# Spatial gating bias: a DVE addition from a copy on every partition in place of one-row TensorE products

## The chip, the cores and the metric

The kernel runs on one core of a Trainium2 chip. The metric is the device time in microseconds. Engines are called PE (TensorE), DVE (VectorE), ACT (ScalarE), POOL (GpSimd) and SP (SyncE). PE writes its products to PSUM, eight banks of 512 fp32 values on each of 128 partitions; the other engines read them from there.

## What is computed

One block of a first network (S5 branch, spatial gating branch, memory attention, feed-forward part) is followed by two layers of a second one (two attentions, a dense feed-forward part, eight experts), for 256 positions of width 1024. The change touches the spatial gating branch only:

```
def sgu_branch(zu, zv, ln_g, ln_b, w_s, bias):
    zu = jax.nn.gelu(zu)
    zv = layer_norm(jax.nn.gelu(zv), ln_g, ln_b)
    zv = zv.reshape(bsz, seq // CHUNK, CHUNK, SGU_HEADS, SGU_HEAD_DIM)
    sv = jnp.einsum('hts,bnshd->bnthd', w_s, zv) + bias.T[None, None, :, :, None]
    return zu * sv.reshape(bsz, seq, SGU_WIDTH)
```

There are 8 heads of 128 columns and 2 chunks of 128 positions. The bias has one number for each head and position, the same for all 128 columns of a head.

## The kernel before

Each engine has one instruction list, written in the order of the computation. The weights come as a stream of 1 MB chunks that SP loads into `ring`, seven slots; PE's first product with a chunk releases a slot, and SP loads the next chunk into it. The results of PE are numbered as units, and unit n lies in PSUM bank n mod 8. `open_unit` waits until the bank's previous unit is free, `close_unit` marks the unit full, `take_unit` waits for that on the engine that reads it, and `free_unit` and `evacuated` signal and wait for the end of the reading. `link` on DVE marks an instruction's end on a semaphore and has DVE wait for it.

Around the change PE runs these stages in order: the transposes and small products of the S5 branch, the projections zu, ga, gb and k (`form_a`, line 657), the projection v (`form_b`, line 683), the spatial gating products (units `sgu` 0 to 3), the projection pb (`form_a`, line 657, with the gated `zuT` as its moving operand), and the y products of the S5 branch (lines 972 to 989). Each projection is four chunks.

The gating works transposed: partitions are the columns of a head, the free axis is the position. A unit `sgu` u holds two heads with two chunks each, four blocks of 128x128. For each block PE makes the product of `zv` with the mixing matrix in `sguT` (L955) and adds to the same bank a product that is one row deep, ones times the bias row `sbias` (L956). `sbias` is one partition of `yaT`, a region that the memory's transpose (`memT`) uses until the projection v has read it, so ACT issues its load (L1466) behind v's last evacuation (L1293). DVE multiplies each unit with `zuT` in place (L2008). Before that, DVE runs the S5 scan (L1984 to L1990, in a loop) up to a small memset (L2001); the scan's data lie in `big`. PE waits for the fourth gated unit before pb.

Of the kernel before, what the change touches and what calls it, by code (L numbers as in the profile page):

```python
# [31 lines left out]
P = 128  # L32
TOK = 256
TB = TOK // P
D = 1024
# [6 lines left out]
ALU = mybir.AluOpType  # L42
# [203 lines left out]
def build(nc, a, out):  # L246
    with ExitStack() as ctx:
# [31 lines left out]
        ones = sb("ones", [P, P])  # L279
# [7 lines left out]
        with ExitStack() as early:  # L287
# [3 lines left out]
            sguT = region("sguT", [P, 8, P])  # L291
            big = region("big", [P, 16384])
# [44 lines left out]
        def view(region, lo, size, pat, **kw):  # L337
# [21 lines left out]
        zv = view(r_zv, 0, 2048, "p (b d) -> p b d", b=TB)  # L359
# [3 lines left out]
        v_t = view(r_v, 0, 2048, "p (b d) -> p b d", b=TB)  # L363
        ygT = memT[:, 0:4, :]
        yaT = memT[:, 4:8, :]
        sbias = yaT.rearrange("p a t -> p (a t)")

        prob = view(r_zv, 0, 1024, "p (n b m) -> p n b m", n=2, b=TB)
        probT = view(r_zv, 1024, 1024, "p (n b l) -> p n b l", n=2, b=TB)
# [31 lines left out]
        loads = {n: sem("ld_" + n) for n in (  # L401
            "x", "mem", "ident", "gains", "prm", "b", "lnv", "sgu", "sbias", "s5d", "cw", "bgate", "sink",
            "nab", "bc0", "ln1", "ln2", "consts")}
# [62 lines left out]
        def bank(u):  # L466
            return psum[:, UNIT_AT[u] % BANKS, :]
# [9 lines left out]
        def take_unit(eng, u):  # L477
            n = UNIT_AT[u]
            eng.wait_ge(bank_full[n % BANKS], n // BANKS + 1)

        def free_unit(last, u):
            last.then_inc(bank_free[UNIT_AT[u] % BANKS], 1)

        def evacuated(eng, u):

            n = UNIT_AT[u]
            eng.wait_ge(bank_free[n % BANKS], n // BANKS + 1)
# [40 lines left out]
        n = 0  # L528
# [89 lines left out]
        def _(pe):  # L618
# [272 lines left out]
            for u in range(8):  # L891
                open_unit(pe, ("t_b", u))
                for j in range(4):
                    n = 4 * (u % 4) + j
                    last = nc.tensor.transpose(bank(("t_b", u))[:, j * P:(j + 1) * P],
                                               b_wide_f[u // 4][:, n * P:(n + 1) * P], ident[:, :])
# [5 lines left out]
            for u0 in range(0, BLK // 2, 4):  # L902
# [3 lines left out]
                for j in range(2):  # L906
                    for r in range(2):
                        for n in (1, 0):

                            for u in group:  # L910
# [6 lines left out]
                                last = nc.tensor.matmul(bank(("bu", u))[:, (2 * j + r) * SCAN:(2 * j + r + 1) * SCAN],  # L917
                                                        bT[n][r0:r0 + 32, r * 8 + blk // 4, :],
                                                        earlier if n else later, start=(n == 1), stop=(n == 0))
# [5 lines left out]
            for d in range(2):  # L925
                for pair in range(PAIRS):
                    i, q = pair % 4, pair // 4
                    for r in range(2):
                        last = nc.tensor.matmul(bank(("kmat", 0))[32 * i:32 * i + 32, (4 * d + q) * 32:(4 * d + q + 1) * 32],
                                                b_wide[0][:, r, d * PAIRS + pair, :, :].rearrange("p g c -> p (g c)"),  # L930
                                                cw[:, r, d * PAIRS + pair, :], start=(r == 0), stop=(r == 1))
# [12 lines left out]

            pe.wait_ge(zvn_ready, 1)
            pe.wait_ge(loads["sgu"], 16)
            pe.wait_ge(loads["sbias"], 16)
            pe.wait_ge(ones_ready, 1)
            for u in range(4):
                open_unit(pe, ("sgu", u))  # L950
                for j in range(2):
                    hd = 2 * u + j
                    for b in range(TB):
                        o = bank(("sgu", u))[:, j * TOK + b * P:j * TOK + (b + 1) * P]
                        nc.tensor.matmul(o, zv[:, b, hd * P:(hd + 1) * P], sguT[:, hd, :], start=True, stop=False)  # L955
                        last = nc.tensor.matmul(o, ones[0:1, :], sbias[0:1, hd * P:(hd + 1) * P],  # L956
                                                start=False, stop=True)
                close_unit(last, ("sgu", u))
            evacuated(pe, ("sgu", 3))
            for i in range(4):  # L960
# [4 lines left out]
            for q in range(4):  # L965
# [3 lines left out]
                for odd in range(2):  # L969
                    for i in range(4):  # L970
                        rows = slice(32 * i, 32 * i + 32)
                        nc.tensor.matmul(out[i][odd], kmat[rows, odd, q, :], uT[rows, q, odd::2],
                                         start=(odd == 0), stop=False, skip_group_check=True)
                for odd in range(2):
                    for r in range(2):
# [5 lines left out]
                        for i in range(4):  # L981

                            fwd, bwd = 4 * q + i, PAIRS + 4 * q + i
                            if odd:
                                last = nc.tensor.matmul(out[i][1][:, 0:SCAN - 1], cw_lam[:, r, bwd, :],
                                                        states[:, SCAN - 2::-1, r, bwd], start=False,
                                                        stop=(r == 1), skip_group_check=True)
                            else:
                                last = nc.tensor.matmul(out[i][0][:, 1:SCAN], cw_lam[:, r, fwd, :],
                                                        states[:, 0:SCAN - 1, r, fwd], start=False,  # L990
                                                        stop=(r == 1), skip_group_check=True)
# [27 lines left out]
            for m in range(2):  # L1019

                for b in range(TB):
# [4 lines left out]
                    for i in range(2):  # L1026
                        if b == 0:
                            open_unit(pe, (f"projb{m}", i))
                        last = split_b_block((f"projb{m}", i), ("k8", f"w_in_{m}", i), b, b)
# [10 lines left out]
                for u in range(3):  # L1040
                    open_unit(pe, (f"t_sw{m}", u))
                    for j in range(2 if u < 2 else 1):
                        for b in range(TB):
                            last = nc.tensor.transpose(
                                bank((f"t_sw{m}", u))[:, (2 * j + b) * P:(2 * j + b + 1) * P],
                                qk_t[:, b, (2 * u + j) * P:(2 * u + j + 1) * P], ident[:, :])
# [39 lines left out]
            for b in range(TB):  # L1086
# [3 lines left out]
                for k in range(KD):  # L1090
                    last = nc.tensor.matmul(bank(("router", 0))[:, b * 8:(b + 1) * 8], xT[:, k, b * P:(b + 1) * P],
                                            wr[:, k, :], start=(k == 0), stop=(k == KD - 1))
# [147 lines left out]
        def _(act):  # L1240
# [198 lines left out]
            for u in range(8):  # L1439
                take_unit(act, ("t_b", u))  # L1440
                n = 4 * (u % 4)
                last = nc.scalar.activation(bT[u // 4][:, n:n + 4, :],
                                            bank(("t_b", u)).rearrange("p (n m) -> p n m", m=P), ACT.Copy)
                free_unit(last, ("t_b", u))
            for u in range(0, BLK // 2, 2):
                take_unit(act, ("bu", u))
                last = nc.scalar.activation(states[:, :, :, bu_block(u):bu_block(u) + 5:4].rearrange("p t r k -> p k r t"),
                                            bank(("bu", u)).rearrange("p (k r t) -> p k r t", k=2, r=2), ACT.Copy)
                free_unit(last, ("bu", u))
            take_unit(act, ("kmat", 0))  # L1450
            last = nc.scalar.activation(kmat[:, :, :, :].rearrange("p d q m -> p (d q m)"),
                                        bank(("kmat", 0))[:, 0:256], ACT.Copy)
            free_unit(last, ("kmat", 0))
            for i in range(4):
                out_of(("zu", i), zuT[:, 2 * i:2 * i + 2, :], ACT.Gelu_apprx_tanh)
            for i in range(4):
# [6 lines left out]
            for i in range(4):  # L1463
                out_of(("v", i), v_t[:, :, i * 256:(i + 1) * 256], ACT.Copy)

            act.dma_start(sbias[0:1, :], a["sgu_bias"]).then_inc(loads["sbias"], 16)  # L1466
            for q in range(4):
                evacuated(act, ("y", q))
                nc.scalar.activation(ygT[:, q, :], ygT[:, q, :], ACT.Gelu_apprx_tanh).then_inc(yg_ready, 1)
            for i in range(2):  # L1470
                take_unit(act, ("glu", i))
                last = nc.scalar.activation(yaT[:, 2 * i:2 * i + 2, :], halves(bank(("glu", i))), ACT.Sigmoid)
# [24 lines left out]
            for m in range(2):  # L1497
# [15 lines left out]
                u = (f"projb{m}", 4)  # L1513
# [3 lines left out]
                last = nc.scalar.activation(v_sw, halves(bank(u))[:, :, 128:256], ACT.Copy)  # L1517
# [19 lines left out]
                for u in range(3):  # L1537
# [3 lines left out]
                    else:  # L1541
                        last = nc.scalar.activation(ksT, bank((f"t_sw{m}", u))[:, 0:TOK], ACT.Copy)
# [94 lines left out]
        def _(dve):  # L1637
# [3 lines left out]
            def link(ins):  # L1641

                steps[0] += 1
                ins.then_inc(dve_step, 1)
                dve.wait_ge(dve_step, steps[0])
# [356 lines left out]


            evacuated(dve, ("zu", 3))
            for u in range(4):
                take_unit(dve, ("sgu", u))
                zs = zuT[:, 2 * u:2 * u + 2, :]
                last = V.tensor_tensor(zs, zs, halves(bank(("sgu", u))), ALU.mult)  # L2008
                free_unit(last, ("sgu", u))
# [429 lines left out]
```

## Time and profile before

| | |
|---|---|
| three runs | 2306.70, 2312.81, 2315.01 us; median 2312.81 |
| profiled execution | 2305.68 us, span 2303.90 us |
| PE busy | 2160.8 us, 94% of the span |
| DVE busy | 1559.0 us, 68% |
| ACT busy | 1193.2 us, 52% |
| granted PE clock, mean | 0.968 of full speed |

PE's lines count two records for each fp32 product. An engine's busy share is a mean over stages with different limits, so the stage around the change is read by itself.

### The profile page before, as it was taken

The page shows a single profiled execution, that of the slowest core. Times are in us where ns is not written, and L with a number is a line of the kernel's source. Part 1 is how long each engine was busy: PE and PEld are TensorE (multiplying, and loading weights), DVE is VectorE, ACT ScalarE, POOL GpSimd, SP SyncE. Part 2 cuts the span into 40 slices and gives each one's busy share as a digit, 9 for nine tenths or more (in the row PEclk, how much of TensorE's full clock was granted, in tenths as well). Part 3 has the DMA queues.
Part 4 walks back from the last instruction along what each step waited for, and adds up shares of the span by engine and source line. Part 5 has one row for each costly group of instructions (what it writes and reads, how often), then busy time and mean ns, then how long its engine had stood idle before and what let it go on. Part 6 is the DMA issues. An engine that isn't in the chain of part 4 may idle for free.

```text
span 2303.9 us, 33192 instructions
## 1 busy us (share of the span) xinstructions
PE 2160.8 (94%) x12622; PEld 1886.0 (82%) x12622; DVE 1559.0 (68%) x1741; ACT 1193.2 (52%) x1203; POOL 9.8 (0%) x22
## 2 busy tenths in 40 slices
PE   6999998799989889998989899999999999999997
PEld 6888778699979688998968788888888888888885
DVE  6775125444554744445474788989898989989897
ACT  2311033344434824343481577777777777777775
POOL 0000000000000000000000000000000000000000
PEclk9999899899999999999999799999999999999998
DMA  7243233245554244555424498989898989989894
GB/s 294 93 149 143 73 121 116 73 166 187 192 205 165 76 145 175 190 184 201 165 74 147 194 372 347 364 343 366 344 366 352 363 344 363 365 345 364 352 358 165
DMA packets 76288, 541.50 MB, mean 235 GB/s; under 512 B 9121, under 2 KB 9265, under 8 KB 11810
## 3 DMA queue, kind: packets, MB, share of 16 engines
q1 hardware_dynamic: 72128, 524.32, 59.2%
q0 software_dynamic: 2080, 10.40, 1.3%
q10 hardware_dynamic: 1986, 5.41, 0.6%
q8 instruction: 73, 1.20, 0.2%
q14 instruction: 21, 0.17, 0.0%
HBM read 539.05 MB, written 1.05 MB: 234 GB/s over the span
## 4 chain that ended last, share of the span: by engine, by line
PE 88%; DVE 6%; ACT 4%; issue 2%; DMA 0%; DVEq 0%; ACTq 0%
PE psum L1173 13%; PE psum L817 11%; PE psum L1150 9%; PE psum L1154 9%; PE psum L1153 9%; PE psum L657 7%; PE psum L716 6%; PE psum L704 6%; PE psum L830 4%; PE psum L670 3%; PE psum L683 2%; PE psum L1116 2%; PE psum L1162 1%; ACT wp_h L1374 1%; PE psum L979 1%
## 5 line engine op out<-in xcount | busy, mean ns | idle before, releaser
L2169 DVE TENSOR_TENSOR w_l<-ring,w_h 128x2048 fp32r<-128x2048 f32 x338 | 773.4, 2290 | 115.9 <-ACT w_h L1360 109.2
L1360 ACT ACTIVATE w_h<-ring 128x2048 fp32r<-128x2048 f32 x338 | 647.6, 1916 | 139.5 <-PE psum L1150 96.1
L1150 PE MATMUL psum<-w_h,xe_h 128*128 128x512 f32 x896 | 360.1, 402 | 2.4 <-DVE xe_l L2253 2.4
L1154 PE MATMUL psum<-w_h,xe_l 128*128 128x512 f32 x896 | 350.8, 391 | 0.0
L1153 PE MATMUL psum<-w_l,xe_h 128*128 128x512 f32 x896 | 350.3, 391 | 0.0
L1820 DVE TENSOR_TENSOR wf_l<-ring,wf_h 128x2048 fp32r<-128x2048 f32 x66 | 151.2, 2291 | 156.9 <-ACT wf_h L1351 156.9
L1794 DVE TENSOR_TENSOR wp_l<-ring,wp_h 128x2048 fp32r<-128x2048 f32 x52 | 119.1, 2292 | 162.3 <-ACT wp_h L1374 162.3
L817 PE MATMUL psum<-xf_h,wf_h 128*128 128x256 f32 x704 | 201.2, 286 | 4.5 <-DVE xf_l L1812 2.5
L817 PE MATMUL psum<-xf_l,wf_h 128*128 128x256 f32 x704 | 200.9, 285 | 0.0
L817 PE MATMUL psum<-xf_h,wf_l 128*128 128x256 f32 x704 | 200.8, 285 | 0.0
L1150 PEld LDWEIGHTS psum<-w_h,xe_h 128*128 128x128 f32 x896 | 168.8, 188 | 38.3 <-DVE w_l L2169 4.0
L1154 PEld LDWEIGHTS psum<-w_h,xe_l 128*128 128x128 f32 x896 | 168.7, 188 | 36.2
L1153 PEld LDWEIGHTS psum<-w_l,xe_h 128*128 128x128 f32 x896 | 169.2, 189 | 32.3
L1351 ACT ACTIVATE wf_h<-ring 128x2048 fp32r<-128x2048 f32 x66 | 125.9, 1910 | 113.7 <-PE psum L830 58.5
L1374 ACT ACTIVATE wp_h<-ring 128x2048 fp32r<-128x2048 f32 x52 | 99.4, 1914 | 145.5 <-PE psum L716 75.2
L817 PEld LDWEIGHTS psum<-xf_h,wf_h 128*128 128x128 f32 x704 | 136.9, 194 | 5.9 <-DVE xf_l L1812 2.8
L1173 PE MATMUL psum<-w_h,eT_h 128*128 128x512 f32 x448 | 140.0, 394 | 0.0
L1173 PE MATMUL psum<-w_h,eT_l 128*128 128x512 f32 x448 | 138.4, 390 | 0.0
L1173 PE MATMUL psum<-w_l,eT_h 128*128 128x512 f32 x448 | 138.2, 390 | 0.0
L817 PEld LDWEIGHTS psum<-xf_l,wf_h 128*128 128x128 f32 x704 | 136.9, 194 | 0.7
L716 PE MATMUL psum<-wp_h,xf_h 128*128 128x256 f32 x384 | 113.1, 295 | 25.7 <-DVE xf_l L1828 12.8
L817 PEld LDWEIGHTS psum<-xf_h,wf_l 128*128 128x128 f32 x704 | 136.8, 194 | 0.0
(366 smaller groups left out, 3721.6 us busy)
## 6 DMA issues: line engine op xcount, KB each, us to landing
ring<-in_stream SPq DMA_DIRECT2D x499, 1024.0 KB, 5.3
big<-in_bc POOLq DMA_DIRECT2D x11, 512.0 KB, 7.0
big<-in_na_bias POOLq DMA_DIRECT2D x2, 2048.0 KB, 9.4
h<-in_x SPq DMA_DIRECT2D x1, 1024.0 KB, 7.2
big<-in_mem ACTq DMA_DIRECT2D x1, 1024.0 KB, 8.6
r_k<-in_sgu_ln ACTq DMA_DIRECT2D x1, 1024.0 KB, 22.5
big<-in_s_c ACTq DMA_DIRECT2D x1, 1024.0 KB, 29.7
out_dram<-ysum ACTq DMA_DIRECT2D x1, 1024.0 KB, 4.1
```

What stands on the lines that cost most here:

```text
L657: last = nc.tensor.matmul(bank(unit)[:, j * TOK:(j + 1) * TOK], w[:, k, j * P:(j + 1) * P], act_T[:, k, :], start=(k == 0), stop=(k == KD ...
L704: last = nc.tensor.matmul(bank(unit)[:, j * TOK:(j + 1) * TOK], w[:, k, j * P:(j + 1) * P], x[:, k, :], start=(k == i == 0), stop=(k == KD ...
L716: last = nc.tensor.matmul(bank(unit)[:, at * 256:(at + 1) * 256], x[:, k, b * P:(b + 1) * P], w[:, k, :], start=(k == i == 0), stop=(k == ...
L817: last = nc.tensor.matmul(psum[:, ff_bank(name, b), j * TOK:(j + 1) * TOK], w[:, k, j * P:(j + 1) * P], x[:, k, :], start=(k == i == 0), s ...
L1150: first = nc.tensor.matmul(out, xe_h[:, k, :], wh[:, i, :], start=(k == 0), stop=False)
L1153: nc.tensor.matmul(out, xe_h[:, k, :], wl[:, i, :], start=False, stop=False)
L1154: last = nc.tensor.matmul(out, xe_l[:, k, :], wh[:, i, :], start=False, stop=(k == KD - 1))
L1173: last = nc.tensor.matmul(psum[:, 4 + c, :], x[:, s % 2, k, :], w[:, k, c * 512:(c + 1) * 512], start=(s == 0 and k == n == 0), stop=(s == ...
L1351: nc.scalar.activation(wf_h[:, n % SPLITS, :], ring[:, at % SLOTS, :], ACT.Copy).then_inc(wf_high, 1)
L1360: nc.scalar.activation(high, src, ACT.Copy).then_inc(w_high, 1)
L1820: V.tensor_tensor(wf_l[:, n % SPLITS, :], ring[:, at % SLOTS, :], wf_h[:, n % SPLITS, :].bitcast(F32), ALU.subtract).then_inc(wf_split, 1)
L2169: V.tensor_tensor(low, src, high.bitcast(F32), ALU.subtract).then_inc(w_split, 1)
```

## The change

The bias is loaded to all 128 partitions, into 1024 columns of `big` that the small S5 products have no more use for, and by ACT ahead of the zu evacuations. PE makes only the sixteen mixing products. DVE adds the bias to each unit in PSUM and then multiplies. PE no longer waits for the bias, DVE does.

```
-        sbias = yaT.rearrange("p a t -> p (a t)")
+        sbias = big[:, 8192:9216].rearrange("p (n m) -> p n m", m=P)
...
             pe.wait_ge(zvn_ready, 1)
             pe.wait_ge(loads["sgu"], 16)
-            pe.wait_ge(loads["sbias"], 16)
             pe.wait_ge(ones_ready, 1)
             for u in range(4):
                 open_unit(pe, ("sgu", u))
                 for j in range(2):
                     hd = 2 * u + j
                     for b in range(TB):
-                        o = bank(("sgu", u))[:, j * TOK + b * P:j * TOK + (b + 1) * P]
-                        nc.tensor.matmul(o, zv[:, b, hd * P:(hd + 1) * P], sguT[:, hd, :], start=True, stop=False)
-                        last = nc.tensor.matmul(o, ones[0:1, :], sbias[0:1, hd * P:(hd + 1) * P],
-                                                start=False, stop=True)
+                        last = nc.tensor.matmul(bank(("sgu", u))[:, j * TOK + b * P:j * TOK + (b + 1) * P],
+                                                zv[:, b, hd * P:(hd + 1) * P], sguT[:, hd, :], start=True, stop=True)
                 close_unit(last, ("sgu", u))
...
             free_unit(last, ("kmat", 0))
+
+            act.dma_start(big[:, 8192:9216], a["sgu_bias"].to_broadcast([P, D])).then_inc(loads["sbias"], 16)
             for i in range(4):
                 out_of(("zu", i), zuT[:, 2 * i:2 * i + 2, :], ACT.Gelu_apprx_tanh)
...
-            act.dma_start(sbias[0:1, :], a["sgu_bias"]).then_inc(loads["sbias"], 16)
             for q in range(4):
                 evacuated(act, ("y", q))
...
             evacuated(dve, ("zu", 3))
+            dve.wait_ge(loads["sbias"], 16)
             for u in range(4):
                 take_unit(dve, ("sgu", u))
+                gate = bank(("sgu", u)).rearrange("p (j b m) -> p j b m", j=2, b=TB)
+                link(V.tensor_tensor(gate, gate, sbias[:, 2 * u:2 * u + 2, :].unsqueeze(2).to_broadcast([P, 2, TB, P]),
+                                     op=ALU.add))
                 zs = zuT[:, 2 * u:2 * u + 2, :]
                 last = V.tensor_tensor(zs, zs, halves(bank(("sgu", u))), ALU.mult)
                 free_unit(last, ("sgu", u))
```

PE, from the end of the projections k and v to the start of pb (`r_zv` holds `zv`, `memT` in L956 is `sbias`, `r_zu` holds `zuT`):

```order
 L657 MATMUL psum<-memT,ring 128x256 x64
 L683 MATMUL psum<-ring,memT 128x256 x64
-L955 MATMUL psum<-sguT,r_zv 128x128
-L956 MATMUL psum<-memT,ones 128x128
...
+L953 MATMUL psum<-sguT,r_zv 128x128 x16
 L657 MATMUL psum<-r_zu,ring 128x256 x64
```

The pair L955, L956 stood sixteen times; sixteen products follow each other now, under the line number 953. Nothing else on PE moves.

DVE, from the end of the scan to the product with pb, before (`r_gb` holds `gbT`):

```order
L1987 TENSOR_TENSOR scan_t<-scan_t 128x64
L1990 TENSOR_TENSOR big<-scan_t,big 128x64
L2001 MEMSET msq 128x2
L2008 TENSOR_TENSOR r_zu<-r_zu,psum 128x512 x4
L2014 TENSOR_TENSOR r_gb<-r_gb,psum 128x512 x4
```

and in the changed kernel:

```order
L1985 TENSOR_TENSOR scan_t<-scan_t 128x64
L1988 TENSOR_TENSOR big<-scan_t,big 128x64
L1999 MEMSET msq 128x2
L2007 TENSOR_TENSOR psum<-psum,big 128x512
L2010 TENSOR_TENSOR r_zu<-r_zu,psum 128x512
...
L2016 TENSOR_TENSOR r_gb<-r_gb,psum 128x512 x4
```

The addition L2007 stands ahead of each of the four products L2010, which were L2008.

ACT, from the last copy of the S5 set-up on, in the changed kernel:

```order
L1444 ACTIVATE big<-psum 128x2x2x128 x8
L1448 ACTIVATE kmat<-psum 128x256
L1452 DMA big<-in_sgu_bias 128x1024
L1290 ACT_TABLE_LOAD
L1290 ACTIVATE r_zu<-psum 128x512 x4
```

The load of the bias stood behind the evacuations of v before, as `memT<-in_sgu_bias` of one row, and now stands ahead of those of zu.

## Rows read from the trace of the kernel before

**Rows 1.** The page: busy time by engine, and the chain by engine.

```profile
PE 2160.8 (94%) x12622; PEld 1886.0 (82%) x12622; DVE 1559.0 (68%) x1741; ACT 1193.2 (52%) x1203; POOL 9.8 (0%) x22
...
PE 88%; DVE 6%; ACT 4%; issue 2%; DMA 0%; DVEq 0%; ACTq 0%
```

**Rows 2.** The chain in order of time: start us, us, what.

```profile
197.82 27.63 PE psum L683 x128
225.44 1.63 issue
...
228.78 0.42 PE psum L955 x2
229.20 0.72 PE psum L956 x2
...
248.76 0.70 DVE r_zu L2008
249.50 29.61 PE psum L657 x128
```

**Rows 3.** The timeline: start us, us, engine, line, what, [idle before it].

```profile
72.11 2.48 DVE L1713 SCALAR_TENSOR_TENSOR r_zv<-r_zv,rstd,r_k 128x1024 f32<-128x1024 f32 x2
...
87.70 1.28 ACT L1293 ACT_TABLE_LOAD   x1
94.25 0.60 ACT L1293 ACTIVATE r_zu<-psum 128x512 f32<-128x512 f32 x1 [5.27 <-PE psum L657]
...
215.78 0.23 DVE L1990 TENSOR_TENSOR big<-scan_t,big 128x64 f32 x1 [0.15 <-DVE scan_t L1987]
...
218.05 0.06 DVE L2001 MEMSET msq<- 128x2 f32 x1
...
225.49 0.49 ACTq L1466 DMA_DIRECT2D memT<-in_sgu_bias  x1
```

**Rows 4.** Groups of instructions, 225.4 to 249.6 us, busy us, mean ns, idle.

```profile
L956 PE MATMUL psum<-memT,ones 1*128 1x128 f32 x32 | 12.1, 475 | 0.0
L955 PE MATMUL psum<-sguT,r_zv 128*128 128x128 f32 x32 | 11.8, 468 | 1.6 <-issue 1.6
...
L2008 DVE TENSOR_TENSOR r_zu<-r_zu,psum 128x512 f32<-128x512 f32 x4 | 2.8, 688 | 28.6 <-PE psum L956 28.6
```

**Rows 5.** Windows: length, PE, PEld, DVE, ACT, POOL busy, clock, DMA share, GB/s.

```profile
227.07:229.12 2.05, 2.05 (x10) 1.45 (x10) 0.00 (x0) 0.31 (x1) 0.00 (x0) 1.00 0.00 0
229.12:248.73 19.61, 19.61 (x55) 13.47 (x54) 2.06 (x3) 0.00 (x0) 0.00 (x0) 0.50 0.00 0
...
249.50:253.00 3.50, 3.50 (x8) 2.86 (x9) 0.00 (x0) 0.00 (x0) 0.00 (x0) 0.50 0.27 61
253.00:279.05 26.05, 26.05 (x122) 22.61 (x120) 2.06 (x3) 0.00 (x0) 0.00 (x0) 1.00 0.42 154
```

**Rows 6.** DMA issues: out<-in, queue, count, KB each, us to landing.

```profile
ring<-in_stream SPq DMA_DIRECT2D x499, 1024.0 KB, 5.3
big<-in_bc POOLq DMA_DIRECT2D x11, 512.0 KB, 7.0
...
r_k<-in_sgu_ln ACTq DMA_DIRECT2D x1, 1024.0 KB, 22.5
```

**Rows 7.** Windows around two later gaps of PE, columns as in rows 5.

```profile
316.00:317.00 1.00, 0.09 (x1) 0.00 (x0) 0.24 (x1) 0.87 (x2) 0.00 (x0) 1.00 0.99 414
317.00:318.00 1.00, 0.49 (x2) 0.47 (x3) 0.45 (x1) 1.00 (x1) 0.00 (x0) 1.00 0.96 386
...
333.00:334.00 1.00, 0.00 (x0) 0.00 (x0) 0.91 (x3) 0.63 (x1) 0.00 (x0) 1.00 0.00 0
...
335.00:336.00 1.00, 1.00 (x7) 1.00 (x7) 0.00 (x0) 0.00 (x0) 0.00 (x0) 0.50 0.00 0
```

**Rows 8.** Groups of instructions, whole span: two of DVE with 128x512 elements.

```profile
L1974 DVE COPY big<-psum 128x512 f32<-128x512 f32 x8 | 9.6, 1310 | 3.3 <-PE psum L917 3.1
...
L1940 DVE TENSOR_TENSOR r_v<-r_zu 128x512 f32<-128x512 f32 x4 | 2.8, 692 | 0.1
```

More of the change, by code:

```diff
@@ L365, in build @@
         yaT = memT[:, 4:8, :]
-        sbias = yaT.rearrange("p a t -> p (a t)")
+        sbias = big[:, 8192:9216].rearrange("p (n m) -> p n m", m=P)
         prob = view(r_zv, 0, 1024, "p (n b m) -> p n b m", n=2, b=TB)
@@ L946, in _ @@
             pe.wait_ge(loads["sgu"], 16)
-            pe.wait_ge(loads["sbias"], 16)
             pe.wait_ge(ones_ready, 1)
@@ L953, in _ @@
                     for b in range(TB):
[L954 to L957, printed above, removed]
+                        last = nc.tensor.matmul(bank(("sgu", u))[:, j * TOK + b * P:j * TOK + (b + 1) * P],
+                                                zv[:, b, hd * P:(hd + 1) * P], sguT[:, hd, :], start=True, stop=True)
                 close_unit(last, ("sgu", u))
@@ L1453, in _ @@
             free_unit(last, ("kmat", 0))
+            act.dma_start(big[:, 8192:9216], a["sgu_bias"].to_broadcast([P, D])).then_inc(loads["sbias"], 16)
             for i in range(4):
@@ L1464, in _ @@
                 out_of(("v", i), v_t[:, :, i * 256:(i + 1) * 256], ACT.Copy)
-            act.dma_start(sbias[0:1, :], a["sgu_bias"]).then_inc(loads["sbias"], 16)
             for q in range(4):
@@ L2004, in _ @@
             evacuated(dve, ("zu", 3))
+            dve.wait_ge(loads["sbias"], 16)
             for u in range(4):
                 take_unit(dve, ("sgu", u))
+                gate = bank(("sgu", u)).rearrange("p (j b m) -> p j b m", j=2, b=TB)
+                link(V.tensor_tensor(gate, gate, sbias[:, 2 * u:2 * u + 2, :].unsqueeze(2).to_broadcast([P, 2, TB, P]),
+                                     op=ALU.add))
                 zs = zuT[:, 2 * u:2 * u + 2, :]
```

## The prediction

> **What bounds the kernel now.** I began with the page's busy table and its chain. TensorE (PE) is busy 94% of the span and carries 88% of the chain, DVE 6% of it [rows 1]. So an instruction taken off PE pays only where PE itself is the chain, and one put on DVE costs only where PE waits for DVE. Next I read the chain around the spatial gating [rows 2]. It runs from the end of the projection of v (L683) at 225.44 us to the first product of the next projection (L657) at 249.50 us, 24.06 us in three pieces:
> - 1.63 us in which PE issues nothing, 225.44 to 227.07. In the timeline [rows 3] the ACT queue issues the one-row load of sgu_bias (L1466) at 225.49, right after PE ended. Of PE's four waits there, the one for `loads["sbias"]` alone has a producer that isn't long done: the layer norm behind `zvn_ready` ended at 74.6 us, and `sguT` and the ones come from the first instructions. The profile doesn't name the releaser ("issue"), so that it is this load is my reading.
> - 21.66 us of 32 products, each of which shows as two PE records. 16 are L955 (the 128x128 mixing matrices), 16 are L956 (the bias, one row deep). The groups show that the two cost the same, 468 and 475 ns a record [rows 4]: the one-row product isn't cheaper for having one row. In the chain a product takes 0.42 us up to 229.20 us, and behind it 27 of them take 229.20 to 248.76, 0.72 us each [rows 2].
> - 0.77 us for the last DVE product of the stage (L2008, 0.69 us) and its two handovers.
>
> The step from 0.42 to 0.72 us is the clock. The granted clock is 1.00 up to 229.12, then 0.50, PE's lower level (1.2 of 2.4 GHz), until 253.00 [rows 5]. Ahead of the fall stood the 1.63 us gap and five products. It rose again 3.5 us into the 256-column products of L657. PE has work without a pause from 229.12 to 248.73, and still the clock stays low.
>
> **The change, part by part.**
>
> *The load moves.* It is issued by ACT behind the kmat copy at about 87.7 us, and PE no longer waits for it. It grows from 4 KB to 512 KB (128 partitions by 4 KB). Loads of that kind and size take 7.0 us to land, and the slowest broadcast of the trace 22.5 us, in the crowd of the first microseconds [rows 6]. DVE wants it after its scan, at 218.05 at the earliest [rows 3]: over 100 us of cover. On ACT the issue lies ahead of a table load at 87.70, and ACT's next evacuation starts at 94.25 [rows 3], so some 5 us of idle time hide it. On the rings it is half of one 1 MB weight chunk; PE eats one chunk per 6.9 us in such a projection (27.63 us for the four of L683) [rows 2] and seven slots stand ahead of it. Cost nothing; if all cover failed, a chunk would be late by about half its 5.3 us [rows 6], 2.7 us. Gain: the 1.63 us.
>
> *Sixteen products leave.* What is left is 16 products of L953. At the upper clock: 16 x 0.42 = 6.7 us. At the lower one throughout: 16 x 0.724 = 11.6 us. Which of them holds is the largest unknown. Before the change PE had the 1.63 us gap and then 2.05 us of this work when the clock fell, 3.68 us after 225.44. Now the work follows the projection without a gap. If the clock fell at the same 229.12 all the same, 8.8 products would be done, and the other 7.2 take 5.2 us: 8.9 us for the sixteen. I take 7.8 us, the middle between never falling (6.7) and falling at the old moment (8.9). For staying up speaks that a later gap of about that length, between 316 and 318 us, didn't bring it down between dense products, while one of nearly 3 us ahead of 334.5 did [rows 7]; for falling speaks that this sparse work never raised it in 19.6 us.
>
> A rule that would shrink this: the Trainium skill gives 134 cycles at the upper clock for 128 columns, 56 ns ("TensorE: Matmul & The Clock Gate", section Back-to-back issue gap), and four passes for true FP32 ("FP8 and Floating Point Precision", section TensorE Precision Notes). That is an estimate of 0.22 us a product; this trace doesn't agree, with 0.42 us. By the Trainium skill's pages the sixteen would be worth 3.6 us.
>
> *Four DVE additions come in.* Each is a 128x512 fp32 tensor_tensor that reads PSUM and the copy (a stride-0 repeat over the two blocks) and writes back to PSUM. Reading PSUM costs nothing extra in the rows (L2008 688 ns), nor does a repeated operand (L1940, 692 ns) [rows 4, 8]. No row of the trace has DVE write PSUM. Below, I bound it by 0.69 us, or 0.60 if it were like ACT's 128x512 evacuations [rows 3]; above, by the slowest group of 128x512 on DVE, the permuting copy L1974 at 1.31 us [rows 8]. I take 0.69, the nearest in shape and operation. The `link` between addition and product costs 0.15 us, the idle ahead of L1990 in the scan, which has the same wait on DVE's own semaphore [rows 3]. A unit thus takes DVE 0.69 + 0.15 + 0.69 = 1.53 us, while PE makes its four products in 1.68 us or more: three of the four pairs lie under PE's work. DVE stands idle for over 28 us of this stage now [rows 4]. Only the last pair is exposed: 0.03 + 1.53 + 0.05 = 1.6 us instead of 0.77. Behind it queue the four products of L2014, which wait for PE anyway. At 1.31 us an addition, DVE would be the pace: first unit ready at 1.68, then 4 x 2.15 us, 10.3 us in all.
>
> *Sum.* Now 24.06 us; after 0 + 7.8 + 1.6 = 9.4 us. Gain 14.7 us, between 15.8 (clock up) and 13.6 (clock falls at the old moment). The projection behind it has about 3.5 us at the lower clock before [rows 5]; with the longer pause of 1.6 us ahead of it I expect about the same. Nothing later reclaims the time: the weight stream is moved by PE's own releases, and its DMA share is 0.42 even behind this stage, at the upper clock [rows 5]. The profiled execution took 2305.68 us (span 2303.90, 1.8 us around it), so 2291.0 us by its own measure. It is at the low end of the runs shown (2306.70 to 2315.01), so against the median of 2312.81 the same gain gives **2298 us**.
>
> **The rivals.**
> - *The clock is low from the first product.* 11.6 + 1.6 = 13.2 us, gain 10.9, 2302 us. For it: in 19.6 us this kind of work never raised the clock. Against it: PE comes out of dense work at 1.00 with no gap. Chance 0.10.
> - *DVE sets the pace,* as PSUM writes are slow. 10.3 us at the upper bound with the clock up, and 8.9 + 2.2 = 11.1 with its fall at the old moment: gain 13.8 or 13.0, about 2299.5 us. For it: the kernel has never had DVE write PSUM. Against it: L2008 and L1940, of the same shape and kind, take 0.69 us whether they read PSUM or SBUF [rows 4, 8]. Chance 0.10.
> - *The products were cheap.* If only the streaming time of a removed product comes back, half of a 256-column product of L683 (27.63 us / 64 = 0.432), that is 16 x 0.216 = 3.5 us, and the gain is 1.63 + 3.5 - 0.83 = 4.3 us: 2308.5 us. Speaks against it that L955 and L956 alternate at equal spacing. The Trainium skill's price of a product gives much the same sum. Chance 0.03.
> - *PE still waits,* since the 1.63 us gap has another cause, such as the switch from one bank to the next. Gain 14.7 - 1.6 = 13.1 us, 2299.7 us. Against it: the chain shows no such gap where one projection follows another. Chance 0.05.
> - *Slower: the clock stays down.* With 6.7 us of sparse work and a longer pause, PE could be at the lower level through the next projection too. At 1.00 that takes about 27.7 us (64 products at 0.432), so at 0.50 it costs 27.7 us more, less the 1.75 us it loses now: 26 us, net 11.3 us slower, 2324 us. It decides from 14.7 us on, that is, from 29 us at the lower clock. Against it: the clock rose 3.5 us into the same products, from the same low level. Chance 0.02.
> - *The gain is there but the whole shows less.* Everything behind moves forward by 15 us and meets the clock's falls at other moments; three runs of the same kernel differ by 8.3 us. Net gain under 11.6 us. Chance 0.12.
>
> My forecast has the rest, 0.58.
>
> **How the numbers follow.** From no change a measurement can tell about 0.5%, 11.6 us. The forecast (0.58) lies above it; so do, with the scatter, 0.08 of the DVE pace, 0.04 of the waiting PE and 0.02 of the low clock: faster 0.72. Same: the rest of those, the cheap products, and the whole that shows less: 0.26. Slower: 0.02. For the range: the gain is 10.9 to 15.8, and up to 17.5 if the next projection loses nothing to the clock; the median of a few runs moves by some 4 us around that. 2312.8 - 17.5 - 4 = 2291 and 2312.8 - 10.9 + 4 = 2306. The forecast's own range is 2293 to 2303.
>
> **What the profile after would show.** No idle time between L683 and L953, and no DMA issue there. 32 records of L953, spaced 0.21 us while the clock reads 1.00 and 0.36 at 0.50; the fall, if there is one, in the middle of them or behind them. L2007 four times at about 0.69 us; each pair but the last inside PE's products. From the end of L683 to the first L657 behind it 8.3 to 10.5 us. The scan and the zu, ga, gb stages unchanged. The prediction is wrong if PE still waits at the start, if L953 runs at 0.36 us from its first record, or if L2007 takes over 1 us.

## The result and the profile after

| | before | after |
|---|---|---|
| six runs each, median | 2310.56 us | 2287.35 us |
| lowest to highest | 2306.47 to 2315.01 | 2285.48 to 2296.66 |
| ratio of the times | | 0.9904 [0.9888, 0.9919] |
| profiled execution | 2305.68 us, span 2303.90 | 2285.48 us, span 2283.7 |
| granted PE clock, mean | 0.968 | 0.974 |
| end of L683 to first L657 of pb | 24.06 us | 6.49 us |

The changed kernel is 0.96% faster by the ratio, 22 us; the two medians are 23.2 us apart. Both are more than the forecast of 14.7 us, and the median lies 3.7 us below the low end of the range of 2291 to 2306 us. The page after, where [rows 1] stood before:

```profile
PE 2140.5 (94%) x12590; PEld 1873.3 (82%) x12590; DVE 1560.0 (68%) x1745; ACT 1193.1 (52%) x1203; POOL 9.8 (0%) x22
```

The chain after, over the stretch of [rows 2] (start us, us, what):

```profile
197.86 27.63 PE psum L683 x128
225.49 0.91 PE psum L953 x8
226.39 0.03 issue
226.42 0.05 DVEq L479
226.47 0.04 issue
226.52 0.71 DVE psum L2007
227.23 0.02 issue
227.25 0.69 DVE r_zu L2010
227.94 0.62 DVE psum L2007
...
231.24 0.70 DVE r_zu L2010
231.94 0.04 issue
231.98 29.58 PE psum L657 x128
```

The pause ahead of the products is gone. Only the first unit of PE is in the chain, and it is there for 0.91 us with four products (eight records). From 226.52 us on the chain is DVE's, four pairs of addition and product at 1.33 us each. The groups between 225.4 and 232.1 us (busy us, mean ns of a record, idle before), where [rows 4] stood:

```profile
L953 PE MATMUL psum<-sguT,r_zv 128*128 128x128 f32 x32 | 3.7, 275 | 0.0
...
L2007 DVE TENSOR_TENSOR psum<-psum,big 128x512 f32<-128x512 f32 x4 | 2.8, 694 | 8.4 <-PE psum L953 8.4
L2010 DVE TENSOR_TENSOR r_zu<-r_zu,psum 128x512 f32<-128x512 f32 x4 | 2.7, 687 | 0.1
```

Sixteen products take 3.7 us by busy time and 3.57 us by the window below, that is 0.22 to 0.23 us each and not 0.42. The mean of a record, 275 ns, is longer than its spacing, since records overlap: a price is read from busy time or from the chain. The windows, to be set beside [rows 5]:

```profile
225.49:229.06 3.57, 3.57 (x32) 3.38 (x31) 2.48 (x4) 1.88 (x2) 0.00 (x0) 1.00 0.00 0
229.06:231.98 2.92, 0.00 (x0) 0.00 (x0) 2.80 (x5) 0.00 (x0) 0.00 (x0) 1.00 0.00 0
231.98:232.86 0.88, 0.88 (x4) 0.80 (x5) 0.00 (x0) 0.00 (x0) 0.00 (x0) 1.00 0.00 0
232.86:236.28 3.42, 3.42 (x10) 2.71 (x9) 0.00 (x0) 0.00 (x0) 0.00 (x0) 0.50 0.64 220
236.28:261.56 25.28, 25.28 (x121) 21.98 (x124) 2.06 (x3) 0.00 (x0) 0.00 (x0) 1.00 0.38 137
```

The granted clock is 1.00 during all sixteen products and during the 2.92 us in which PE waits for DVE. It falls 0.9 us into pb and is up again 3.42 us later. The load of the bias, in the table of DMA issues:

```profile
big<-in_sgu_bias ACTq DMA_DIRECT2D x1, 512.0 KB, 4.4
```

It is issued at 87.20 us and lands 4.4 us later, far ahead of the addition at 226.52.

### The profile page after: what moved, and what is told of

Read it like the earlier page. It is cut to its first block, busy times and chain, and to the rows that moved or that the text cites. A ratio compares the mean times of both kernels' runs of the same rounds, so it can differ in the third digit from the quotient of the medians.

```text
span 2283.7 us, 33132 instructions
## 1 busy us (share of the span) xinstructions
PE 2140.5 (94%) x12590; PEld 1873.3 (82%) x12590; DVE 1560.0 (68%) x1745; ACT 1193.1 (52%) x1203; POOL 9.8 (0%) x22
## 3 DMA queue, kind: packets, MB, share of 16 engines
HBM read 539.57 MB, written 1.05 MB: 237 GB/s over the span
## 4 chain that ended last, share of the span: by engine, by line
PE 87%; DVE 6%; ACT 4%; issue 2%; DMA 0%; DVEq 0%; ACTq 0%
PE psum L1170 13%; PE psum L817 11%; PE psum L1147 9%; PE psum L1151 9%; PE psum L1150 9%; PE psum L657 7%; PE psum L716 6%; PE psum L704 6%; PE psum L830 4%; PE psum L670 3%; PE psum L683 2%; PE psum L1113 2%; PE psum L1159 1%; ACT wp_h L1371 1%; PE psum L976 1%
## 5 line engine op out<-in xcount | busy, mean ns | idle before, releaser
L1150 PE MATMUL psum<-w_l,xe_h 128*128 128x512 f32 x896 | 350.5, 391 | 0.0
L1818 DVE TENSOR_TENSOR wf_l<-ring,wf_h 128x2048 fp32r<-128x2048 f32 x66 | 151.2, 2291 | 156.1 <-ACT wf_h L1348 156.1
L1792 DVE TENSOR_TENSOR wp_l<-ring,wp_h 128x2048 fp32r<-128x2048 f32 x52 | 119.1, 2291 | 160.7 <-ACT wp_h L1371 160.7
L1150 PEld LDWEIGHTS psum<-w_l,xe_h 128*128 128x128 f32 x896 | 169.2, 189 | 32.3
L716 PE MATMUL psum<-wp_h,xf_h 128*128 128x256 f32 x384 | 112.3, 293 | 25.4 <-DVE xf_l L1826 12.5
```

The lines of the kernel that those rows point to most:

```text
L716: last = nc.tensor.matmul(bank(unit)[:, at * 256:(at + 1) * 256], x[:, k, b * P:(b + 1) * P], w[:, k, :], start=(k == i == 0), stop=(k == ...
L1150: nc.tensor.matmul(out, xe_h[:, k, :], wl[:, i, :], start=False, stop=False)
L1818: V.tensor_tensor(wf_l[:, n % SPLITS, :], ring[:, at % SLOTS, :], wf_h[:, n % SPLITS, :].bitcast(F32), ALU.subtract).then_inc(wf_split, 1)
```

## The experiments

"Stage" means from the end of L683 to the first L657 of pb: 24.06 us before, 6.49 us after. A ratio is against the kernel before, timed on the same chip. The first question was why a product of L953 costs 0.22 to 0.23 us and not 0.42.

**The load alone.** The kernel before, with its one-row load moved; the sixteen one-row products stay.

```
-        sbias = yaT.rearrange("p a t -> p (a t)")
+        sbias = big[:, 8192:9216]
...
+            act.dma_start(sbias[0:1, :], a["sgu_bias"]).then_inc(loads["sbias"], 16)
             for i in range(4):
                 out_of(("zu", i), zuT[:, 2 * i:2 * i + 2, :], ACT.Gelu_apprx_tanh)
...
-            act.dma_start(sbias[0:1, :], a["sgu_bias"]).then_inc(loads["sbias"], 16)
```

> Only the load moves: one row of the bias goes to its new place in big ahead of the zu evacuations, PE still makes the sixteen pairs. Measured from the end of L683 to the first L657 behind it (24.06 us before, 6.49 in the changed kernel). If the 1.63 us gap was the wait for this load: no gap. If the gap has another cause: it stays. The 32 products then take 13.4 us if the clock stays at its upper level (0.42 us each), and up to about 20 if it falls some microseconds into them; so 14.2 to 21 us in all, and a whole that is 3 to 10 us below before.

Measured: 2308.14 us, ratio 0.9983 [0.9966, 1.0000]. The products follow L683 with no idle time, so the 1.63 us were the wait for the load. The chain at their start:

```profile
226.16 0.22 PE psum L955 x2
226.38 0.41 PE psum L956 x2
226.80 0.42 PE psum L955 x2
```

The first product of L955 stands behind L683, which is 128 rows deep like itself, and costs 0.22 us; the same instruction behind a one-row product costs 0.42.

The stage takes 19.4 us. Of the 4.7 us saved, 1.6 are the wait and 0.2 the first product (0.46 us behind the pause, 0.22 here). Nearly all of the rest is that the clock fell later: 5.6 us after the end of L683, with no pause ahead. Two windows of this kernel (columns as in rows 5):

```profile
226.16:231.80 5.64, 5.64 (x30) 3.95 (x28) 0.69 (x1) 1.88 (x2) 0.00 (x0) 1.00 0.00 0
231.80:245.55 13.75, 12.97 (x36) 8.86 (x36) 2.06 (x3) 0.00 (x0) 0.00 (x0) 0.50 0.00 0
```

So the clock falls in the alternating products without a pause ahead of them too. The time of the whole, expected 3 to 10 us lower, fell by 2.7 us between medians, with an interval that reaches to no change.

**The bias product with 128 rows.** Still sixteen bias products on PE, each as deep as the mixing product: a 128x128 matrix of 1/128 (`mean`) times the bias on every partition. DVE makes no addition, and fills the matrix behind its scan, at about 218 us, in time for PE.

```
-        sbias = yaT.rearrange("p a t -> p (a t)")
+        sbias, mean = big[:, 8192:9216], big[:, 9216:9344]
...
+            act.dma_start(sbias, a["sgu_bias"].to_broadcast([P, D])).then_inc(loads["sbias"], 16)
...
-                        last = nc.tensor.matmul(o, ones[0:1, :], sbias[0:1, hd * P:(hd + 1) * P],
+                        last = nc.tensor.matmul(o, mean, sbias[:, hd * P:(hd + 1) * P],
```

> Sixteen pairs on PE as before, no DVE addition, but the bias product is as deep as the other: a matrix of 1/128 times the copy of the bias on every partition, which sums to the bias. Theory A, the change of depth between 128 rows and one costs about 0.19 us at each product: 32 products at 0.23 us, 7.3 + 0.8 = 8.1 us for the stage, and the whole within 2 us of the changed kernel. Rival B, a product that adds to the block just written has to wait for it: 32 at 0.42, 14.2 us or more, the whole 8 us or more above the changed kernel.

Measured: 2294.47 us, ratio 0.9943 [0.9923, 0.9963]. Its chain:

```profile
227.44 0.22 PE psum L956 x2
...
228.11 0.23 PE psum L957 x2
...
234.18 0.70 DVE r_zu L2009
...
234.92 25.09 PE psum L657 x115
```

32 products, as many as before, take 7.2 us in place of 21.7. Each costs 0.22 us and the clock reads 1.00 from L683 through pb. The number of products was never the cost, and neither is adding to the block just written (rival B): each bias product does that here.

The stage came out as expected, at 7.9 us. The whole did not: it was expected within 2 us of the changed kernel and is slower, at a ratio of 0.9943 against 0.9904, though stage and pb together take 35.8 us here and 36.1 there. In the profiled executions this kernel is 9.2 us longer, and 7.5 of these lie behind the first product of the next attention (L716), in code that is the same. More on that stretch stands below.

**Grouped by depth, one-row products kept.** With the early load, each unit makes its four mixing products and then its four one-row products.

```
-                        nc.tensor.matmul(o, zv[:, b, hd * P:(hd + 1) * P], sguT[:, hd, :], start=True, stop=False)
-                        last = nc.tensor.matmul(o, ones[0:1, :], sbias[0:1, hd * P:(hd + 1) * P],
+                for n, (j, b, o) in enumerate(blocks):
+                    nc.tensor.matmul(o, zv[:, b, hd * P:(hd + 1) * P], sguT[:, hd, :], start=(n == 0), stop=False,
...
+                for n, (j, b, o) in enumerate(blocks):
+                    last = nc.tensor.matmul(o, ones[0:1, :], sbias[0:1, hd * P:(hd + 1) * P], start=False,
```

> One-row bias products, early load, but in each unit the four 128-row products first and then the four one-row ones: 8 changes of depth in place of 32. Theory A (a price for each change of depth): 7.3 + 8 x 0.19 + 0.8 = 9.6 us for the stage. Rival B (a product waits for the one that wrote its block): each block is written four products apart, 8.1 us. Rival C (the one-row product is dear by itself, 0.42 x 2 - 0.23 = 0.61 us): 3.7 + 9.8 + 0.8 = 14.3 us.

Measured: 2299.52 us, ratio 0.9953 [0.9935, 0.9971]. Its chain, four products (eight records) to a row:

```profile
226.95 0.89 PE psum L955 x8
227.84 1.08 PE psum L959 x8
228.92 1.09 PE psum L955 x8
230.01 1.08 PE psum L959 x8
231.09 1.91 PE psum L955 x8
233.01 2.00 PE psum L959 x8
```

The first four cost 0.89 us. Each later group costs 0.19 to 0.20 us more, once, for the change of depth ahead of it; 0.19 + 0.22 is the 0.41 of the alternating order. At the lower clock, from about 231.2 us on, the group takes 2.00 us. Four one-row products in a row take 1.08 us, so such a product isn't dear by itself (rival C, 0.61 us each). The stage takes 12.8 us; the 9.6 us of the price for a change of depth were worked out for a clock that stays up.

**One one-row product for a unit.** As before, but the four one-row products of a unit are one, with 512 columns.

```
-                for n, (j, b, o) in enumerate(blocks):
-                    last = nc.tensor.matmul(o, ones[0:1, :], sbias[0:1, hd * P:(hd + 1) * P], start=False,
+                last = nc.tensor.matmul(bank(("sgu", u)).rearrange("p (j b m) -> p j b m", j=2, b=TB), ones[0:1, :],
+                                        row.unsqueeze(2).to_broadcast([1, 2, TB, P]), start=False, stop=True,
```

> Early load of one row, no DVE addition, and in each unit the four 128-row products and then a single one-row product over all 512 columns (2 changes of depth a unit, 4 bias products in place of 16). By a price of 0.19 us for each change of depth: 3.7 + 4 x 0.86 + 8 x 0.19 + 0.8 = 9.4 us for the stage with the clock up. The kernel with 128-row bias products kept the upper clock through 7 us, the grouped one with one-row products lost it after 4 us. Theory D, one-row products by themselves bring the clock down, however dense their columns: it falls here too, some microseconds in, although PE streams columns nearly all the time. Rival E, it is the thin spacing of columns: the clock stays up.

Measured: 2294.55 us, ratio 0.9929 [0.9906, 0.9952]. The two kinds take 1.05 and 1.09 us in turn, the stage 9.1 us. The clock stayed up through all of them, 8.4 us, and fell at about 235.5 us, 0.4 us into the pause ahead of pb. The 128-row kernel has the same pause of 0.8 us and no fall in it. So one-row products didn't bring the clock down while they ran; whether the fall right behind them is theirs is open.

**How deep is deep enough.** The 128-row experiment once more with 100, 64 and 32 rows of both operands, and 1/rows in the matrix. All else is as there.

```
-                        last = nc.tensor.matmul(o, mean, sbias[:, hd * P:(hd + 1) * P],
+                        last = nc.tensor.matmul(o, mean[0:100, :], sbias[0:100, hd * P:(hd + 1) * P],
```

> The bias products alternate with the 128-row products and are 100 rows deep. Between 128-row products (0.22 us each) and one-row ones (0.42 us) lies a rule to be found. Theory F, the price is for another set of 32-row groups: 100 rows use all four, so 0.22 us a product, 7.2 us for 32. Rival G, any change of depth costs: 0.42 us a product, 13.4 us.

> The same with bias products 64 rows deep, two of the four 32-row groups. Theory F and rival G both say 0.42 us a product. If the price grows as the depth differs more, about 0.3 us.

> The same with bias products 32 rows deep, one group, as the one-row product has. 0.42 us a product if the group counts; if it is something of the single row itself, 0.22 us.

Measured, in a single run each: 2285.27, 2296.43 and 2310.23 us, where the kernel before took 2306.14 us. These times carry little; the chains carry the verdict. The chain with 100 rows:

```profile
225.73 0.22 PE psum L956 x2
225.95 0.22 PE psum L957 x2
```

With 64 rows:

```profile
226.40 0.41 PE psum L957 x2
226.81 0.42 PE psum L956 x2
```

With 32 rows, where the clock's fall shows as well:

```profile
226.16 0.41 PE psum L957 x2
226.58 0.42 PE psum L956 x2
...
229.49 0.65 PE psum L957 x2
```

| rows of the bias product | us a product, clock 1.00 | stage | clock |
|---|---|---|---|
| 128 | 0.22 | 7.9 us | 1.00 throughout |
| 100 | 0.22 | 7.9 us | 1.00 throughout |
| 64 | 0.42 | 13.9 us | 1.00 through the stage, fell 0.4 us into pb |
| 32 | 0.42 | 20.9 us | fell 3.6 us in |
| 1 (load alone) | 0.42 | 19.4 us | fell 5.6 us in |

The step lies between 64 and 100 rows. TensorE's rows come in four groups of 32 in the Trainium skill ("TensorE: Matmul & The Clock Gate", section Terms). 100 rows touch all four groups, as 128 do; 64 touch two, and 32 or 1 touch one. A price for any difference in depth would have 100 rows beside 128 cost more, and they don't; a price that grows with the difference would have 64 rows cost less than one, and they don't. A price for different groups fits all five rows of the table. It isn't the only thing that fits: no run has 65 to 99 rows, so any other limit between 64 and 100 rows would give the same table. 96 rows, three groups, would tell.

The timeline shows what goes with it. Before the change, weight load (PEld) and product of L956 stand at the same moment:

```profile
227.46 0.29 PEld L956 LDWEIGHTS psum<-memT,ones 1*128 1x128 f32 x2
227.46 0.48 PE L956 MATMUL psum<-memT,ones 1*128 1x128 f32 x2
```

and after the change the loads run ahead of the products:

```profile
225.11 3.76 PEld L953 LDWEIGHTS psum<-sguT,r_zv 128*128 128x128 f32 x32
225.32 3.73 PE L953 MATMUL psum<-sguT,r_zv 128*128 128x128 f32 x32
```

With 128 and 100 rows each load leads its product by 0.11 us; with 64 and 32 rows it doesn't. Before the change the load of L956 starts at 227.46 us, when the record of the product ahead (L955, 0.46 us from 227.07) has 0.07 us to go. The same page of the Trainium skill, in Part 3, section The mechanism, says that PE pulls a weight load ahead of running products when its row groups don't conflict with theirs or when it goes to the background buffer. The trace agrees for neighbours of 128 rows and for 100 beside 128, where the loads run ahead. That the load for a product of 64, 32 or 1 rows beside 128 doesn't, at about 0.2 us a change, is what the runs here show. That the missing lead is the cause of the price is my reading of the two together.

**No additions.** The changed kernel without its four additions; it leaves the bias out.

```
-                gate = bank(("sgu", u)).rearrange("p (j b m) -> p j b m", j=2, b=TB)
-                link(V.tensor_tensor(gate, gate, sbias[:, 2 * u:2 * u + 2, :].unsqueeze(2).to_broadcast([P, 2, TB, P]),
-                                     op=ALU.add))
```

> The changed kernel without the four DVE additions: it leaves out the bias. In the changed kernel DVE sets the pace of the stage with four pairs of 1.33 us behind the first unit. Without the additions PE's sixteen products (3.7 us) set it: 3.7 + 0.8 = 4.5 us in place of 6.49, so the additions cost 2.0 us. Rival: the pause ahead of pb is what brings the clock down; with 0.8 us of it in place of 3, pb no longer runs 3.4 us at the lower level, and another 1.7 us come back.

Measured: 2288.16 us, ratio 0.9910 [0.9891, 0.9928].

```profile
224.35 3.59 PE psum L953 x32
...
227.96 0.70 DVE r_zu L2007
...
228.70 27.89 PE psum L657 x128
```

The stage takes 4.35 us and pb runs at 1.00 throughout, 27.89 us in place of 29.58. So the additions cost 2.1 us of stage and 1.7 us in pb. The whole kernel isn't faster than the changed one: what is won here didn't reach the end in these runs. Where it was lost in the profiled execution is said below.

**The load back at its old place.** The changed kernel, with the 512 KB load behind v's last evacuation.

```
-            act.dma_start(big[:, 8192:9216], a["sgu_bias"].to_broadcast([P, D])).then_inc(loads["sbias"], 16)
             for i in range(4):
                 out_of(("zu", i), zuT[:, 2 * i:2 * i + 2, :], ACT.Gelu_apprx_tanh)
...
+            act.dma_start(big[:, 8192:9216], a["sgu_bias"].to_broadcast([P, D])).then_inc(loads["sbias"], 16)
```

> The changed kernel with its 512 KB load back at the old place, behind the evacuation of v. PE's products don't wait for it, DVE's first addition does: issue at 225.5 and 2.5 to 5 us to land, so the first addition starts at 228 to 230.5 in place of 226.5 and the stage takes 8 to 10.5 us in place of 6.5. It gives what moving the load is worth once the bias is DVE's. Rival: below 1 us, as four units' products hide it.

Measured: 2293.25 us, ratio 0.9922 [0.9899, 0.9946].

```profile
226.26 3.69 DMA big<-in_sgu_bias
...
230.02 0.71 DVE psum L2006
...
235.49 24.52 PE psum L657 x101
```

The stage takes 9.3 us, 2.8 more. Now the profile names the load in the chain. The clock falls in the longer pause and stays low for 5.0 us of pb.

**PE waits unit by unit.** If DVE is the pace, pb needn't wait for the fourth gated unit at once. The first group of pb waits for one unit ahead of every two of its eight products.

```
-            evacuated(pe, ("sgu", 3))
...
+                        if unit == ("pb", 0) and j == 0 and k % 2 == 0:
+                            evacuated(pe, ("sgu", k // 2))
```

> The changed kernel, but the first product group of pb waits for each gated unit where it reads it, not for the fourth before it starts. PE's pause of 3 us ahead of pb shrinks to under 0.5 us: 6 of its 64 products (2.6 us) move ahead of the last DVE product. Theory: the fall of the clock behind that pause goes as well, 3.4 us at the lower level, another 1.7 us; about 4 us below the changed kernel in the stage. In the whole this may be hidden, since runs of one kernel differ by several us with the moments at which the clock falls later. Rival: DVE's chain is the bound, and PE waits as long in four pieces: no gain.

> The changed kernel once more, on the chip of these runs, as their measure: 2285 to 2292 us, 0.9904 of before. If the gain of 22 us is 17.6 us in the stage and a little less time at the lower clock elsewhere, span times granted clock falls by 6 to 8 us against before, and the time not at full clock by the rest.

Measured on one chip: 2288.11 us, ratio 0.9905 [0.9883, 0.9927], and for the changed kernel 2288.59 us, ratio 0.9908 [0.9888, 0.9928]. PE in the timeline of the new one:

```profile
229.11 2.89 PE L659 MATMUL psum<-r_zu,ring 128*128 128x256 f32 x12
232.20 4.15 PE L659 MATMUL psum<-r_zu,ring 128*128 128x256 f32 x18 [0.20 <-DVE r_zu L2011]
```

The pause of 2.9 us is filled, the clock reads 1.00 from 225.7 to 260 us, and pb ends at 257.50 us, where it ends at 261.78 in the changed kernel profiled beside it: 4.3 us earlier. The two medians can't be told apart all the same, with six runs of each that spread over 13.6 and 10.5 us. In the two profiled executions the gain is still there at the end, 2283.39 against 2288.94 us. The repeated changed kernel gave the expected time; its span multiplied by the granted clock lies 5.6 us below that of the kernel before, where 6 to 8 were expected.

## Why the prediction was right or wrong

**The load.** Right. The pause was the wait for it, as the load-alone experiment shows, and its cover held.

**"Sixteen products leave".** This step failed, in the price of the sixteen that stay. I had them at 0.42 us, 6.7 to 11.6 us in all and 7.8 in the sum. They took 3.7 us. I read the 0.42 us of [rows 2] as the price of a product, since L955 and L956 cost the same. It is the price of a product behind one of another depth, 0.22 + 0.2 us, and all but the first of the 32 in the old order paid it. Removing the one-row products halved the cost of the others too. In the comparison of the Trainium skill's 0.22 us with the 0.42 us of the trace I gave way to the row. The measured 0.22 us between products of equal depth agrees with the estimate, and the row showed another condition. The rival "The products were cheap" took a cheap product for a small gain, and that is wrong as well: a product that costs 0.22 us behind one of its own depth cost 0.42 in the old order.

**The clock in the products.** I expected it to stay up or to fall midway. It stayed at 1.00, so the moment of 229.12 was not fixed. In the old order it fell after 2.1 us of products behind a pause, and after 5.6 us with none. With 32 full-depth products over 7.2 us it didn't fall. Staying up was within my range, but none of my rows chose between the two cases, and I took the middle.

**"Three of the four pairs lie under PE's work".** Wrong, as a consequence. It rested on 1.68 us for a unit's products, and a unit takes 0.9 us. DVE's pair, at 1.33 us, sets the pace, and the chain is DVE's from the end of PE's first unit at 226.39 to 231.94 us. PE waits 2.9 us behind its last product, where I had 1.6. The rival "DVE sets the pace" was right in its name and wrong in its cause. This write to PSUM isn't slow: L2007 takes 0.694 us, as I had it. The handover between addition and product costs 0.02 us in the chain, not the 0.15 us of the short scan instructions; with the overlap of records, a pair repeats in 1.33 us and not 1.53.

**The stage.** Predicted 0 + 7.8 + 1.6 = 9.4 us. Measured 0.91 of PE, 0.13 of handover, 5.42 of DVE and 0.04 back to PE: 6.5 us. The gain there is 17.6 us, not 14.7. With 3.7 us for the products and the last pair alone exposed it would have been 5.3 us: one error took 4.1 us too many, the other gave 1.2 back. The experiment without additions, at 4.35 us, shows that the wait for DVE is the additions' doing.

**pb.** Right. It starts 17.5 us earlier, and its time at the lower clock is 3.4 us, where it was 3.5, behind a pause of 2.9 us.

**The whole.** The miss of the whole has three parts, and only one of them, the stage, comes from the steps above. The forecast of 2298 us lies some 11 us above the median of 2287.35. 2.3 of them come from the kernel before, whose median of six runs is 2310.56 and not the 2312.81 of three. 2.9 are the stage, 17.6 and not 14.7 us; by it alone the result would have been 2295 us. 5.6 us, 23.2 less 17.6, lie outside the stage.

Between the two profiled executions the gain is 20.2 us. In these two, the first product of the next attention (L716) starts 18.0 us earlier and ends its first stretch 19.5 us earlier. The chains there:

before:

```profile
334.48 24.79 PE psum L716 x192
```

after:

```profile
316.51 23.30 PE psum L716 x192
```

Before, the clock fell inside this stretch (0.84 on average in its first 10.5 us); after, it read 1.00, with the same code. That this belongs to the change is not shown. Between the first product of L716 and the first one with the experts' weights (L1150 in the kernel before), which every kernel here computes alike, the profiled executions took 956 to 969 us, a scatter larger than those 5.6 us, while from there to the end all took 1011 us. The scatter is the clock's: the time missing at the lower clock, added up over windows of 1 us, is 44 to 59 us of that stretch, and what remains of it is 908 to 913 us in all thirteen executions. The kernel without additions started L716 5.0 us before the changed one and took 10.4 us longer up to the experts. What sets the moments of these falls is open. The range should have been wider for them: its low end allowed 4 us for the scatter of medians and no more than 17.5 us of gain.

In terms of the clock: over the 27 runs of the kernel before and the 12 of the changed one whose clock is known, the span multiplied by the granted clock fell from 2230.5 to 2225.2 us, and the span multiplied by what was missing of it from 77.5 to 61.9. Of the 21 us, 5 are work and waits counted at full speed, and 16 are time no longer missing at the lower clock. By this count 10.2 of these are in the stage itself: half of the 20.4 us from 229.12 to 249.50. It is a count and not a price: at the lower clock a product took 0.72 us and not twice 0.42, and the fall cost the 32 products 8.4 us.

## What to carry to other kernels

Read a product's price with its neighbour: in this kernel a thin product cost twice, by its own 0.22 us and by the change of depth on either side of it, 0.2 us each. So try to group products by depth, or make a thin one as deep as its neighbours (here 32 full-depth products took 7.2 us, and 16 full with 16 thin ones 21.7, 13.3 by the price of 0.42 us and 8.4 more by the clock's fall), before moving the work elsewhere. When work is taken off one engine, work out the other's pace again, from the new spacing and not the old. And where the granted clock falls at several later places, a gain of under 5 us has to be looked for in its stage, since here medians of four to six runs didn't show it.

## What was not expected of the hardware

- A change between products of 128 rows and of 64, 32 or 1 rows costs 0.19 to 0.20 us at a clock of 1.00, and the weight loads no longer run ahead there. 100 rows beside 128 don't pay it. Where between 64 and 100 rows the limit lies wasn't measured.
- Busy PE is not enough for the clock. With PE busy without a pause it fell in the alternating orders of 1 and 32 rows (after 5.6 and 3.6 us) and in the grouped one-row order (after 4.2 us). With 64 rows, at the same 0.42 us a product, it stayed up for 13.1 us of products and fell behind a pause of 0.8 us, 0.4 us into pb; with 100 and 128 rows the same pause brought no fall. What tells these apart is left open.
- An elementwise DVE operation that writes PSUM, 128x512 fp32, takes 0.694 us, as one that writes SBUF does.
